# A diffusion layer on one core: the turn from the mixer into the FFN, token tile by token tile

## The chip, the core and the metric

One Trainium2 chip, one of its cores. The core has TensorE (PE, the matrix engine, with its weight loads shown as PEld), VectorE (DVE), ScalarE (ACT), GpSimd (POOL) and SyncE (SP, which here issues the large loads). The engines run their own instruction streams in order and meet through semaphores. The metric is the device time of one launch in microseconds. A run's time is a little longer than the span from its first to its last profiled instruction.

## What is computed

One layer of a diffusion backbone over 256 latent tokens and 256 context tokens of width 2048. The part that this case is about begins at the output projection:

```
x = x + g1 * rms_norm(mix @ w_out, mix_norm_post)
hf = rms_norm(x, ffn_norm_pre) * (1 + sc2) + sh2
x = x + g2 * rms_norm((silu(hf @ w_gate) * (hf @ w_up)) @ w_down, ffn_norm_post)
```

`mix` is what the mixer (gated DeltaNet heads and a conformer branch) leaves, and `g1`, `sc2`, `sh2`, `g2` are columns of a modulation computed from the conditioning vector. `w_out` is 2048 by 2048, `w_gate` and `w_up` are 2048 by 5632, `w_down` is 5632 by 2048. All data are float32.

## The kernel before

**Products in three parts.** Every large product is made of float32r matmuls. Each operand is split into a rounded part (`_hi`) and the remainder (`_lo`), and a product is hi by hi, hi by lo and lo by hi: `product()` (L1774 to L1779) issues three matmuls of 128x512. ScalarE makes the rounded part by a copy (L924), VectorE the remainder by a subtraction (L1325, L1358).

**Weights in units.** Weights come in units of 128 partitions by 1024 columns (512 KB, two k tiles by 512 output columns) through four slots of `raw`, `w_hi` and `w_lo` (`RING = 4`). SP loads a unit as soon as the unit four before it has been split into both parts. A unit can be split into `w_hi` when TensorE has finished the unit four before it. One unit is 12 matmuls on TensorE for the two token tiles (t = 0 and 1, 128 tokens each) and two k tiles.

**The order.** For the mixer and the turn into the FFN there is one list of steps, `PLAN`, built by `make_plan()`. Each engine walks through the whole list and issues the steps that are its own, so the list sets the order on every engine at once. A step waits for others by `need(engine, kind, key)`, a semaphore wait on the count of that kind. Behind the list, each engine runs the FFN loop `gate_up(c, ...)` over 11 chunks of 512 columns, eight units of `w_gate` and eight of `w_up` each, and then the units of `w_down`.

**The turn into the FFN.** Output projection units are named `("wo", c, kg)`: column group c (0 to 3) of 512 columns, kg one of 8 pairs of k tiles. The last column group, c = 3, ends with kg = 0, 1, 2, 3. Token tile t of column group c is accumulated in the PSUM bank 2c + t. Behind it stand these steps:

- `ysq` (ACT, L1205) squares and sums a bank, `ysm` (DVE, L1682) adds the four sums, `yrt` (ACT, L1209) takes the root, `yrc` (DVE, L1686) the reciprocal. `yg` (DVE, L1678) multiplies a bank by the gate and norm weights. `ysq` and `yg` of c = 0 to 2 are done beside the projection.
- `pn` (DVE, L1696) adds the normed bank to the residual `x1`, 8 pieces of 128x512 (t, c).
- `psq` (ACT, L1227), `psm` (DVE, L1682), `xrt` (ACT, L980), `xrc` (DVE, L1363) do the same for the second norm. `xdg` (DVE, L1367) puts the reciprocals on the diagonals `dg`, the matmul `xT` with kp = 8 (PE, L1888) spreads them over the partitions, and `xTc` (ACT, L924) copies them into `rsb`.
- `xT` with kp = 0 to 7 (PE, L1784) transposes `x1`: four 128x128 transposes for each pair kp of k tiles, both token tiles.
- Then for each kp: `fx` (DVE, L1375) multiplies the transposed bank by `rsb` into `hf2`; `fm` (ACT, L1236, two instructions) applies scale and shift in place; `fhi` (ACT, L924) rounds into `h_hi`; `flo` (DVE, L1380) writes the remainder `h_lo`. `hf2` has two buffers, so `fx` of kp waits for `flo` of kp - 2.
- `fh` and `fl` are the two splits of FFN weight unit i (ACT L924, DVE L1325). 0 to 6 stand in the list, the rest in `gate_up`. Unit i = kp of the FFN on TensorE needs `flo` of kp and both splits.

In this version each of these steps serves both token tiles, and the norm of token tile 0 waits for the end of the whole projection: `need(act, "mm", ("wo", c, 3), QS - 1)`. GpSimd does nothing behind its last mixer step but one load of `x1`.

## Time and profile before

| | us |
|---|---|
| median of 3 runs | 1640.35 |
| lowest and highest | 1638.05, 1641.5 |
| the profiled execution | 1639.05 |
| its span | 1637.3 |
| granted TensorE clock, mean over the span | 0.986 |

In the profile an engine's busy time is the union of its instructions. Durations of matmuls are modelled at their ends, so the pace of a stream of matmuls is read from start to start. A row of the timeline gives start, length, engine, line, operation and tiles, the number of instructions merged into it, and in brackets how long the engine had been idle before and what ended that. Tile names in the profile leave out numbers: `x` is `x1`, `hf` is `hf2`, `junk` is `junk2`, `sc` is `sc2`.

### The profile page before, as it was taken

The page shows a single profiled execution, that of the slowest core. Times are in us where ns is not written, and L with a number is a line of the kernel's source. Part 1 is how long each engine was busy: PE and PEld are TensorE (multiplying, and loading weights), DVE is VectorE, ACT ScalarE, POOL GpSimd, SP SyncE. Part 2 cuts the span into 40 slices and gives each one's busy share as a digit, 9 for nine tenths or more (in the row PEclk, how much of TensorE's full clock was granted, in tenths as well). Part 3 has the DMA queues.
Part 4 walks back from the last instruction along what each step waited for, and adds up shares of the span by engine and source line. Part 5 has one row for each costly group of instructions (what it writes and reads, how often), then busy time and mean ns, then how long its engine had stood idle before and what let it go on. Part 6 is the DMA issues. An engine that isn't in the chain of part 4 may idle for free.

```text
span 1637.3 us, 25093 instructions
## 1 busy us (share of the span) xinstructions
PE 1545.0 (94%) x9295; PEld 1298.1 (79%) x9295; DVE 1046.0 (64%) x1446; ACT 768.8 (47%) x1044; POOL 227.5 (14%) x236
## 2 busy tenths in 40 slices
PE   4887999998989999999998999999999999999998
PEld 0557888887878898898876888888888888888886
DVE  1436798999996857675565645544544455777554
ACT  5526633443345645457355644444344444443342
POOL 2000232333332333244200000000000000000000
PEclk9998999999999999999999999999999999999999
DMA  9993555655554555564464666666666665999654
GB/s 355 395 382 97 172 182 184 197 177 196 168 177 158 168 187 196 170 208 130 142 220 127 184 190 192 187 186 190 192 192 186 188 190 176 336 324 322 229 183 139
DMA packets 190977, 334.58 MB, mean 204 GB/s; under 512 B 14706, under 2 KB 80354, under 8 KB 189985
## 3 DMA queue, kind: packets, MB, share of 16 engines
q1 hardware_dynamic: 190194, 330.89, 62.8%
q0 software_dynamic: 688, 2.39, 0.5%
q8 instruction: 63, 1.03, 0.3%
q14 instruction: 32, 0.26, 0.0%
HBM read 331.15 MB, written 2.10 MB: 204 GB/s over the span
## 4 chain that ended last, share of the span: by engine, by line
PE 78%; DVE 11%; DMA 4%; ACT 3%; issue 2%; SPq 2%; DVEq 0%; ACTq 0%
PE PS L1778 64%; DMA first<-in_w_mod_dram 3%; DVE cacc L1639 3%; DVE w_lo L1358 3%; PE PS L1784 2%; PE PS L2086 2%; PE PS L2040 2%; PE PS L1992 2%; SPq L711 2%; DVE sil L1467 1%; PE PS L1938 1%; DVE gh L1525 1%; PE PS L1982 1%; PE PS L1873 1%; DVE xyi L1530 1%
## 5 line engine op out<-in xcount | busy, mean ns | idle before, releaser
L924 ACT ACTIVATE w_hi<-raw 128x1024 fp32r<-128x1024 f32 (+1 forms) x426 | 448.1, 1056 | 513.4 <-PE PS L1778 430.4
L1325 DVE TENSOR_TENSOR w_lo<-raw,w_hi 128x1024 fp32r<-128x1024 f32 x264 | 322.9, 1225 | 316.6 <-ACT w_hi L924 316.5
L1778 PE MATMUL PS<-w_hi,h_hi 128*128 128x512 f32 x704 | 275.0, 391 | 1.9 <-DVE h_lo L1380 1.2
L1778 PE MATMUL PS<-w_hi,h_lo 128*128 128x512 f32 x704 | 274.0, 389 | 0.0
L1778 PE MATMUL PS<-w_lo,h_hi 128*128 128x512 f32 x704 | 273.9, 389 | 0.0
L1358 DVE TENSOR_TENSOR w_lo<-raw,w_hi 128x1024 fp32r<-128x1024 f32 (+1 forms) x162 | 201.4, 1252 | 70.5 <-ACT w_hi L924 70.5
L1778 PE MATMUL PS<-h_hi,w_hi 128*128 128x256 f32 (+1 forms) x784 | 237.6, 303 | 0.0
L1778 PE MATMUL PS<-h_hi,w_lo 128*128 128x256 f32 (+1 forms) x784 | 222.0, 283 | 0.0
L1778 PE MATMUL PS<-h_lo,w_hi 128*128 128x256 f32 (+1 forms) x784 | 221.9, 283 | 0.0
L1778 PEld LDWEIGHTS PS<-h_hi,w_hi 128*128 128x128 f32 (+1 forms) x784 | 148.9, 190 | 36.0 <-issue 27.6
L1778 PEld LDWEIGHTS PS<-w_hi,h_hi 128*128 128x128 f32 x704 | 132.1, 188 | 29.5 <-DVE h_lo L1380 1.4
L1778 PEld LDWEIGHTS PS<-w_hi,h_lo 128*128 128x128 f32 x704 | 132.1, 188 | 27.6
L1778 PEld LDWEIGHTS PS<-w_lo,h_hi 128*128 128x128 f32 x704 | 132.2, 188 | 27.1
L1778 PEld LDWEIGHTS PS<-h_lo,w_hi 128*128 128x128 f32 (+1 forms) x784 | 149.1, 190 | 0.8
L1778 PEld LDWEIGHTS PS<-h_hi,w_lo 128*128 128x128 f32 (+1 forms) x784 | 148.5, 189 | 0.1
L1778 PE MATMUL PS<-w_hi,act_hi 128*128 128x512 f32 x352 | 137.9, 392 | 0.0
L1778 PE MATMUL PS<-w_hi,act_lo 128*128 128x512 f32 x352 | 137.0, 389 | 0.0
L1778 PE MATMUL PS<-w_lo,act_hi 128*128 128x512 f32 x352 | 136.9, 389 | 0.0
L1639 DVE SCALAR_TENSOR_TENSOR cacc<-ub,vcol,cacc 128x196 f32<-128x196 f32 (+14 forms) x240 | 126.2, 585 | 0.2
L873 POOL TENSOR_TENSOR mkl<-kc,lvl 128x512 fp32r<-128x512 f32 x56 | 83.4, 1489 | 155.4 <-PE PS L1982 118.9
L1778 PE MATMUL PS<-hc_hi,w_hi 128*128 128x256 f32 (+1 forms) x272 | 83.8, 308 | 11.5 <-ACT w_hi L924 4.2
L1467 DVE SCALAR_TENSOR_TENSOR sil<-PS,vcol,sil 128x254 f32<-128x254 f32 (+1 forms) x160 | 76.6, 480 | 16.0 <-ACT sil L1044 11.7
(322 smaller groups left out, 2353.7 us busy)
## 6 DMA issues: line engine op xcount, KB each, us to landing
raw<-in_w_in_dram SPq DMA_DIRECT2D x128, 512.0 KB, 3.9
raw<-in_w_mod_dram SPq DMA_DIRECT2D x96, 512.0 KB, 5.0
raw<-in_w_gate_dram SPq DMA_DIRECT2D x88, 512.0 KB, 3.7
raw<-in_w_up_dram SPq DMA_DIRECT2D x88, 512.0 KB, 3.7
raw<-in_w_down_dram SPq DMA_DIRECT2D x88, 512.0 KB, 4.5
first<-in_w_mod_dram SPq DMA_DIRECT2D x64, 512.0 KB, 9.6
raw<-in_w_out_dram SPq DMA_DIRECT2D x32, 512.0 KB, 4.3
gin<-in_w_mod_dram SPq DMA_DIRECT2D x32, 512.0 KB, 6.0
```

What stands on the lines that cost most here:

```text
L711: sp.dma_start(first[:, slot, :].rearrange("p (a b) -> p a b", a=2), w_mod_v[:, 2 * j:2 * j + 2, part * D + q * 512:part * D + (q + 1) * 5 ...
L873: pool.tensor_tensor(mkl[:, :, :, :].rearrange("p t h c -> p (t h) c"), kc[:, :, :, :].bitcast(F32).rearrange("p t h c -> p (t h) c"), bc( ...
L924: act.activation(out_ap, in_ap, ACT.Copy).then_inc(S[kind], 1)
L1325: dve.tensor_tensor(w_lo[:, slot, :], raw[:, (R0 + n) % RING, :], w_hi[:, slot, :].bitcast(F32), ALU.subtract).then_inc(S["lo"], 1)
L1358: dve.tensor_tensor(lo, raw[:, at_ring[u] % RING, 0:sz], hi.bitcast(F32), ALU.subtract).then_inc(done, 1)
L1467: ins = dve.scalar_tensor_tensor(out=o, in0=pr[:, T * h + a + off:T * h + b + off], scalar=vcol[:, col:col + 1], in1=o, op0=ALU.mult, op1= ...
L1639: ins = dve.scalar_tensor_tensor(out=dst, in0=src, scalar=vcol[:, col:col + 1], in1=dst, op0=ALU.mult, op1=ALU.add)
L1778: ins = pe.matmul(out_ap, a[i], b[j], start=start and n == 0, stop=stop and n == 2, skip_group_check=grouped)
L1784: ins = pe.transpose(PS[:, bank_, P * n:P * (n + 1)], src, ident[:, :])
L1992: ins = pe.matmul(PS[:, b, P * n:P * (n + 1)], a, m, start=False, stop=True, skip_group_check=True)
L2040: ins = pe.matmul(PS[:, b, P * n:P * (n + 1)], a, m, start=True, stop=True)
L2086: ins = pe.matmul(PS[32 * tile:32 * tile + 1, 3, :], csil[:, LAT, j:j + 1], raw[:, n % RING, 512 * h:512 * (h + 1)], start=j == 0, stop=j ...
```

## The change

The first norm, the second norm, the transposes and the modulation are made for token tile 0 and token tile 1 apart. The last four projection units (c = 3, kg = 0 to 3) first run their token tile 0 halves (parts 0 and 2 of each), all four, and then, in the new list, their token tile 1 halves (parts 1 and 3); `ysq 0 3` waits for the token tile 0 halves alone. The steps of the turn are no longer built by loops but read from a written list `INTO_FFN`, 148 steps, in which the third token of an `xT`, `fx`, `fm`, `fhi`, `flo` is the token tile. `fx`, `fhi` and `flo` become twice as many instructions of 128x(2x128), `fm` twice as many of 128x128. FFN units 0 to 3 are computed by a new step `ft` on TensorE, one for each unit and token tile (6 matmuls). The remainders of FFN weight units 1 to 3 are made by GpSimd in a new step `gl`; each waits for the rounding of its own unit and for the remainder before it, and VectorE's remainder of unit 4 waits for the last of them.

Transposed pairs now use half a bank for each pair: kp 0 and 1 of tile t in bank 6 + t, kp 2 and 3 in 2 + t, 4 and 5 in 4 + t, 6 and 7 in 6 + t again. `xT` of kp 6 and 7 waits for both `fx 0` and `fx 1` of its tile.

```diff
-TURNED = (6, 7, 2, 3, 4, 5, 6, 7, 1)
+TURNED = (6, 6, 2, 2, 4, 4, 6, 6, 0)
+BY_TILE = 4
...
-        unit(("wo", c, kg), QS)
+        u = ("wo", c, kg)
+        if c == 3 and kg < BY_TILE:
+            plan.extend([("hi", (u,)), ("lo", (u,))] + [("mm", (u, half * NT)) for half in range(2)])
+            continue
+        unit(u, QS)
...
-    plan.extend([(k, (i,)) for i in range(3) for k in ("fh", "fl")])
-    plan.extend([("ysq", (t, 3)) for t in range(NT)] + [("ysm", ()), ("yrt", ()), ("fh", (3,))])
-    plan.extend([("yg", (t, 3)) for t in range(NT)] + [("yrc", ())])
-    plan.extend([(k, (t, c)) for c in (3, 0, 1, 2) for t in range(NT) for k in ("pn", "psq")])
-    plan.extend([("xT", (FFN, kp)) for kp in range(6)])
-    plan.extend([("psm", ()), ("xrt", (FFN,)), ("xrc", (FFN,)), ("xdg", ())])
-    plan.extend([("xT", (FFN, 8)), ("xTc", (FFN, 8)), ("fx", (FFN, 0)), ("fm", (FFN, 0)), ("fhi", (FFN, 0)), ("fx", (FFN, 1)),
-                 ("xT", (FFN, 6)), ("xT", (FFN, 7))])
-    for kp in range(8):
-        plan.append(("flo", (FFN, kp)))
-        plan.extend([("fm", (FFN, kp + 1)), ("fhi", (FFN, kp + 1))] if kp < 7 else [])
-        plan.extend([("fx", (FFN, kp + 2))] if kp < 6 else [])
-        if kp == 1:
-            plan.append(("fl", (3,)))
-        elif kp in SPLIT_AT:
-            plan.extend([("fh", (SPLIT_AT.index(kp) + 4,)), ("fl", (SPLIT_AT.index(kp) + 4,))])
+    plan.extend(into_ffn())
...
+INTO_FFN = """
+    ysq 0 3, ysm 0, yrt 0, yg 0 3, yrc 0, mm 0 1, mm 0 3, mm 1 1, xT 0 0, mm 1 3, mm 2 1, mm 2 3, mm 3 1, mm 3 3,
+    xT 8 0, xT 1 0, fh 0, pn 0 3, psq 0 3, pn 0 0, psq 0 0, fh 1, pn 0 1, psq 0 1, pn 0 2, psq 0 2, ysq 1 3, psm 0,
...
+                elif kind == "gl":
+                    i, = key
+                    pool.wait_ge(S["hi"], B0 + i + 1)
+                    pool.wait_ge(S["lo"], B0 + i)
+                    slot = (B0 + i) % RING
+                    pool.tensor_tensor(w_lo[:, slot, :], raw[:, (R0 + i) % RING, :], w_hi[:, slot, :].bitcast(F32),
+                                       ALU.subtract).then_inc(S["lo"], 1)
...
-                    need(act, "mm", ("wo", c, 3), QS - 1)
-                    n = COUNT[kind, key] - 1
+                    need(act, "mm", ("wo", c, 3), NT + t)
+                    n = SQUARED.index((kind, key))
                     if n >= 4:
-                        act.wait_ge(S[kind], n - 3)
+                        need(act, SQUARED[n - 4][0], *SQUARED[n - 4][1])
...
+                    _, kp, t = key
+                    need(act, "fx", FFN, kp, t)
                     need(act, "s2")
                     for k in range(2):
                         kt = 2 * kp + k
-                        ins = act.activation(hf2[:, kp % 2, k, :], hf2[:, kp % 2, k, :], ACT.Identity, scale=sc2[:, kt:kt + 1],
+                        part = hf2[:, kp % 2, k, P * t:P * (t + 1)]
+                        ins = act.activation(part, part, ACT.Identity, scale=sc2[:, kt:kt + 1],
                                              bias=modc[:, KT + kt:KT + kt + 1])
                     ins.then_inc(S[kind], 1)
                 elif kind == "fhi":
-                    _, kp = key
-                    need(act, "fm", FFN, kp)
-                    copy(h_hi[:, 2 * kp:2 * kp + 2, :], hf2[:, kp % 2, :, :], kind)
+                    _, kp, t = key
+                    need(act, "fm", FFN, kp, t)
+                    tok = slice(P * t, P * (t + 1))
+                    copy(h_hi[:, 2 * kp:2 * kp + 2, tok], hf2[:, kp % 2, :, tok], kind)
...
+                if n == BY_TILE:
+                    dve.wait_ge(S["lo"], B0 + n)
...
-                    need(dve, "xrc", FFN)
-                    for t in range(NT):
-                        ins = dve.tensor_scalar(dg[:, t, :], ident[:, :], rstd[:, 4 + t:5 + t], None, ALU.mult)
-                    ins.then_inc(done, 1)
+                    t, = key
+                    need(dve, "xrc", FFN, t)
+                    dve.tensor_scalar(dg[:, t, :], ident[:, :], rstd[:, 4 + t:5 + t], None, ALU.mult).then_inc(done, 1)
                 elif kind == "fx":
-                    _, kp = key
-                    need(dve, "xT", FFN, kp)
-                    need(dve, "xTc", FFN, 8)
+                    _, kp, t = key
+                    need(dve, "xT", FFN, kp, t)
+                    need(dve, "xT", FFN, kp ^ 1, t)
+                    need(dve, "xTc", FFN, 8, t)
                     if kp >= 2:
-                        need(dve, "flo", FFN, kp - 2)
-                    dve.tensor_tensor(hf2[:, kp % 2, :, :], PS[:, TURNED[kp], :].rearrange("p (k t) -> p k t", k=2),
-                                      bc(rsb[:, :], 1, 2), ALU.mult).then_inc(done, 1)
+                        need(dve, "flo", FFN, kp - 2, t)
+                    tok = slice(P * t, P * (t + 1))
+                    src = PS[:, TURNED[kp] + t, T * (kp % 2):T * (kp % 2 + 1)].rearrange("p (k t) -> p k t", k=2)
+                    dve.tensor_tensor(hf2[:, kp % 2, :, tok], src, bc(rsb[:, tok], 1, 2), ALU.mult).then_inc(done, 1)
                 elif kind == "flo":
-                    _, kp = key
-                    need(dve, "fhi", FFN, kp)
-                    dve.tensor_tensor(h_lo[:, 2 * kp:2 * kp + 2, :], hf2[:, kp % 2, :, :],
-                                      h_hi[:, 2 * kp:2 * kp + 2, :].bitcast(F32), ALU.subtract).then_inc(done, 1)
+                    _, kp, t = key
+                    need(dve, "fhi", *key)
+                    tok = slice(P * t, P * (t + 1))
+                    dve.tensor_tensor(h_lo[:, 2 * kp:2 * kp + 2, tok], hf2[:, kp % 2, :, tok],
+                                      h_hi[:, 2 * kp:2 * kp + 2, tok].bitcast(F32), ALU.subtract).then_inc(done, 1)
...
-                    need(dve, *(("ysq", 1, 3) if kind == "ysm" else ("psq", 1, 2)))
-                    a, o = (8, 6) if kind == "ysm" else (16, 4)
-                    dve.tensor_reduce(sums[:, o:o + 2], sums[:, a:a + 8].rearrange("p (t c) -> p t c", t=NT), AX_X,
-                                      ALU.add).then_inc(done, 1)
+                    t, = key
+                    need(dve, *(("ysq", t, 3) if kind == "ysm" else ("psq", t, 2)))
+                    a, o = (8 + 4 * t, 6 + t) if kind == "ysm" else (16 + 4 * t, 4 + t)
+                    dve.tensor_reduce(sums[:, o:o + 1], sums[:, a:a + 4], AX_X, ALU.add).then_inc(done, 1)
...
+                    if key[0] == FFN:
+                        _, kp, t = key
+                        b = TURNED[kp] + t
+                        if kp == 8:
+                            need(pe, "xdg", t)
+                            need(pe, "pn", t, 0)
+                            pe.matmul(PS[:, b, 0:P], ones[:, :], dg[:, t, :], start=True, stop=True).then_inc(done, 1)
+                            continue
+                        need(pe, "pn", t, kp // 2)
+                        if kp < 2:
+                            need(pe, "pn", t, 3)
+                        if kp >= 6:
+                            need(pe, "fx", FFN, 0, t)
+                            need(pe, "fx", FFN, 1, t)
+                        for k in range(2):
+                            ins = pe.transpose(PS[:, b, T * (kp % 2) + P * k:T * (kp % 2) + P * (k + 1)],
+                                               x1[:, t, P * (2 * kp + k):P * (2 * kp + k + 1)], ident[:, :])
+                        ins.then_inc(done, 1)
+                        continue
...
+                elif kind == "ft":
+
+                    i, t = key
+                    slot, tok = (B0 + i) % RING, slice(P * t, P * (t + 1))
+                    pe.wait_ge(S["hi"], B0 + i + 1)
+                    pe.wait_ge(S["lo"], B0 + i + 1)
+                    need(pe, "flo", FFN, i, t)
+                    need(pe, "xTc", FFN, 8, t)
+                    for k in range(2):
+                        col, kt = slice(512 * k, 512 * (k + 1)), 2 * i + k
+                        ins = product(PS[:, t, :], (h_hi[:, kt, tok], h_lo[:, kt, tok]), (w_hi[:, slot, col], w_lo[:, slot, col]),
+                                      512, kt == 0, False)
+                    if t == NT - 1:
+                        ins.then_inc(f_mm, 1)
...
+                        if i < BY_TILE:
+                            continue
                         if i < 8:
-                            need(pe, "flo", FFN, i)
-                            need(pe, "xTc", FFN, 8)
+                            for t in range(NT):
+                                need(pe, "flo", FFN, i, t)
```

ScalarE, from the squares of the last projection bank on. Before (`w_hi<-raw` are weight splits, `junk2,sums` are `ysq` on a bank and `psq` on `x1`, the `rtmp` rows `yrt` and `xrt`):

```order
L1205 ACTIVATE junk2,sums<-PS 128x512 x2
L1209 ACTIVATE rtmp<-sums,cst 128x2
L924 ACTIVATE w_hi<-raw 128x1024
L1227 ACTIVATE junk2,sums<-x1 128x512 x8
L980 ACTIVATE rtmp<-sums,cst 128x2
L924 ACTIVATE rsb<-PS 128x256
L1236 ACTIVATE hf2<-hf2,modc,sc2 128x256 x2
L924 ACTIVATE h_hi<-hf2 128x512
```

and now:

```order
L1236 ACTIVATE junk2,sums<-PS 128x512
L1241 ACTIVATE rtmp<-sums,cst 128x1
L950 ACTIVATE w_hi<-raw 128x1024
L1256 ACTIVATE junk2,sums<-x1 128x512 x2
L950 ACTIVATE w_hi<-raw 128x1024
L1256 ACTIVATE junk2,sums<-x1 128x512 x2
L1236 ACTIVATE junk2,sums<-PS 128x512
L1011 ACTIVATE rtmp<-sums,cst 128x1
L1241 ACTIVATE rtmp<-sums,cst 128x1
L950 ACTIVATE rsb<-PS 128x128
L950 ACTIVATE w_hi<-raw 128x1024
L1266 ACTIVATE hf2<-hf2,modc,sc2 128x128 x2
```

Three weight splits (units 0, 1 and 2) that stood ahead of the first row before now stand behind it, between the steps of the two norms, and the root of token tile 0's second norm stands behind the square of token tile 1's last projection bank.

VectorE, from the sum of `ysq` to the first `h_lo`. Before:

```order
L1682 TENSOR_REDUCE sums<-sums 128x2
L1678 TENSOR_TENSOR PS<-PS,gw_all 128x512 x2
L1686 RECIPROCAL rstd<-rtmp 128x2
L1696 SCALAR_TENSOR_TENSOR x1<-PS,rstd,x1 128x512 x8
L1682 TENSOR_REDUCE sums<-sums 128x2
L1363 RECIPROCAL rstd<-rtmp 128x2
L1367 TENSOR_SCALAR dg<-ident,rstd 128x128 x2
L1375 TENSOR_TENSOR hf2<-PS,rsb 128x512 x2
L1380 TENSOR_TENSOR h_lo<-hf2,h_hi 128x512
```

and now, from the second sum of token tile 0 on:

```order
L1719 TENSOR_REDUCE sums<-sums 128x1
L1358 TENSOR_TENSOR w_lo<-raw,w_hi 128x1024
L1719 TENSOR_REDUCE sums<-sums 128x1
L1714 TENSOR_TENSOR PS<-PS,gw_all 128x512
L1397 RECIPROCAL rstd<-rtmp 128x1
L1723 RECIPROCAL rstd<-rtmp 128x1
L1401 TENSOR_SCALAR dg<-ident,rstd 128x128
L1733 SCALAR_TENSOR_TENSOR x1<-PS,rstd,x1 128x512
L1411 TENSOR_TENSOR hf2<-PS,rsb 128x2x128 x2
L1733 SCALAR_TENSOR_TENSOR x1<-PS,rstd,x1 128x512 x2
L1416 TENSOR_TENSOR h_lo<-hf2,h_hi 128x2x128
```

The remainder of weight unit 0 and token tile 1's first norm now stand between the second sum of token tile 0 and its diagonal.

TensorE, at the end of the projection (`hc_` operands) and the start of the FFN (`h_` operands). Before:

```order
L1778 MATMUL PS<-w_hi,hc_lo 128x512
L1784 MATMUL PS<-ident,x1 128x128 x24
L1888 MATMUL PS<-dg,ones 128x256
L1784 MATMUL PS<-ident,x1 128x128 x8
L1778 MATMUL PS<-w_hi,h_hi 128x512
```

and now, where the last projection matmul is followed by:

```order
L1815 MATMUL PS<-w_hi,hc_lo 128x512
L1926 MATMUL PS<-dg,ones 128x128
L1935 MATMUL PS<-ident,x1 128x128 x14
L1815 MATMUL PS<-w_hi,h_hi 128x512
```

Two transposes of token tile 0 (`xT 0 0`) are moved up into the projection, 15 matmuls (two and a half units' token tile 1 halves) ahead of its end, and the other 14 of that tile stand behind the matmul that needs the diagonal; the 16 of token tile 1 are spread among the `ft` steps.

## Rows read from the trace of the kernel before

**Rows 1.** The page: busy time by engine; a weight load with its time to landing.

```profile
PE 1545.0 (94%) x9295; PEld 1298.1 (79%) x9295; DVE 1046.0 (64%) x1446; ACT 768.8 (47%) x1044; POOL 227.5 (14%) x236
...
raw<-in_w_gate_dram SPq DMA_DIRECT2D x88, 512.0 KB, 3.7
```

**Rows 2.** The chain of waits behind the turn: start, length, engine and line.

```profile
912.00 46.50 PE PS L1778 x204
```

**Rows 3.** Timeline of TensorE through the turn.

```profile
882.35 0.39 PE L1778 MATMUL PS<-w_hi,hc_lo 128*128 128x512 f32 x1
...
888.33 4.76 PE L1784 MATMUL PS<-ident,x 128*128 128x128 f32 x24 [5.59 <-DVE x L1696]
...
895.02 1.23 PE L1784 MATMUL PS<-ident,x 128*128 128x128 f32 x8 [1.36 <-DVE hf L1375]
897.44 0.50 PE L1778 MATMUL PS<-w_hi,h_hi 128*128 128x512 f32 x1 [1.20 <-DVE h_lo L1380]
...
912.00 0.47 PE L1778 MATMUL PS<-w_hi,h_hi 128*128 128x512 f32 x1 [0.66 <-DVE w_lo L1325]
```

**Rows 4.** Stretches: length, busy time (instructions) by engine, granted clock, DMA.

```profile
882.80:912.00 29.20, 20.46 (x95) 16.87 (x95) 20.57 (x34) 23.46 (x50) 0.00 (x0) 0.88 0.20 57
...
885.40:888.30 2.90, 0.00 (x0) 0.00 (x0) 2.87 (x7) 2.08 (x7) 0.00 (x0) 0.51 0.08 30
888.30:892.20 3.90, 3.87 (x18) 3.87 (x19) 2.77 (x5) 3.66 (x12) 0.00 (x0) 0.50 0.00 0
892.20:893.70 1.50, 1.46 (x10) 0.94 (x8) 0.65 (x3) 0.00 (x1) 0.00 (x0) 0.97 0.00 0
```

**Rows 5.** Groups of instructions from 882 to 914 us, ScalarE: busy, mean ns.

```profile
L1236 ACT ACTIVATE hf<-hf,modc,sc 128x256 f32<-128x256 f32 x16 | 8.7, 591 | 2.7 <-DVE hf L1375 2.7
...
L924 ACT ACTIVATE w_hi<-raw 128x1024 fp32r<-128x1024 f32 x5 | 5.1, 1043 | 0.0
L924 ACT ACTIVATE h_hi<-hf 128x512 fp32r<-128x512 f32 x8 | 5.1, 632 | 0.3
L1227 ACT ACTIVATE junk<-x 128x512 f32<-128x512 f32 x8 | 5.0, 631 | 0.8 <-DVE x L1696 0.8
```

**Rows 6.** The same groups, VectorE.

```profile
L1375 DVE TENSOR_TENSOR hf<-PS,rsb 128x512 f32<-128x512 f32 x8 | 5.4, 690 | 2.1 <-ACT rsb L924 1.3
L1380 DVE TENSOR_TENSOR h_lo<-hf,h_hi 128x512 fp32r<-128x512 f32 x8 | 5.4, 685 | 1.4 <-ACT h_hi L924 1.2
L1696 DVE SCALAR_TENSOR_TENSOR x<-PS,rstd,x 128x512 f32<-128x512 f32 x8 | 5.4, 741 | 0.0
```

**Rows 7.** Timeline of ScalarE and VectorE through the turn.

```profile
882.78 0.60 ACT L1205 ACTIVATE junk<-PS 128x512 f32<-128x512 f32 x1 [1.60 <-PE PS L1778]
...
885.55 5.36 DVE L1696 SCALAR_TENSOR_TENSOR x<-PS,rstd,x 128x512 f32<-128x512 f32 x8
...
894.91 1.09 ACT L1236 ACTIVATE hf<-hf,modc,sc 128x256 f32<-128x256 f32 x2 [0.83 <-DVE hf L1375]
...
896.03 0.63 ACT L924 ACTIVATE h_hi<-hf 128x512 fp32r<-128x512 f32 x1
...
896.57 1.08 ACT L1236 ACTIVATE hf<-hf,modc,sc 128x256 f32<-128x256 f32 x2
...
911.60 0.63 ACT L924 ACTIVATE h_hi<-hf 128x512 fp32r<-128x512 f32 x1
```

**Rows 8.** Groups of ScalarE over the span, small pieces: busy, mean ns.

```profile
L1131 ACT ACTIVATE gmv<-kn 128x128 f32<-128x128 f32 x32 | 9.5, 297 | 0.2
```

**Rows 9.** One line each: durations min/median/max in ns, first and last start.

```profile
L880 POOL TENSOR_TENSOR mlo<-mn,mhi x16: 1288/1402/1737, 230.7 to 784.1; 128x512 fp32r<-128x512 f32 x16
...
L1637 DVE TENSOR_SCALAR cacc<-ub,vcol x8: 338/348/1385, 158.2 to 422.2; 128x256 f32<-128x256 f32 x8
```

**Rows 10.** Timeline of GpSimd and VectorE at 561 us.

```profile
560.91 1.28 POOL L873 TENSOR_TENSOR mkl<-kc,lvl 128x512 fp32r<-128x512 f32 x1 [6.55 <-DVE pi L1512]
561.04 2.24 DVE L1358 TENSOR_TENSOR w_lo<-raw,w_hi 128x1024 fp32r<-128x1024 f32 x1 [0.20 <-ACT w_hi L924]
```

88 lines of the change are left out of this document (50 added, 38 removed).

## Prediction

> **What bounds the kernel now.** I read the page first, then the chain of waits, then the turn into the FFN engine by engine. TensorE is busy for 94% of the span [rows 1], and from 912.00 us on the chain is TensorE alone, 204 matmuls in 46.50 us [rows 2], 0.227 us from start to start, 2.72 us for a unit of 12. So before and behind the turn the kernel is bound by TensorE, and the change can move the end only by moving the moment from which TensorE streams without a gap. I take the start of FFN unit 8 as the mark, the first that needs weights alone. Five units (0 to 4) are computed before 912.00, so it now starts at 912.00 + 3 x 2.72 = 920.16.
>
> The last projection matmul ends at 882.35 + 0.39 = 882.74 [rows 3]. In the 37.4 us from there to the mark TensorE must do 8 units, 21.8 us, and 32 transposes; 8 of them at full clock took 1.23, so all take at most 4.9. The rest, 10.7 us, is all that a perfect turn could give back (0.65%). The timeline names 8.8 of it: 5.59 waiting for the residual, 1.36 for `fx`, 1.20 for the first remainder, 0.66 for the remainder of weight unit 5 [rows 3]. The clock has most of the rest: from 885.4, 2.7 us behind the last matmul, to 892.2 the granted clock is 0.5, its 1.2 GHz level, and 24 transposes take 4.76 [rows 3, 4].
>
> The engine next to the limit is ScalarE. In the 29.2 us of the turn it is busy for 23.46, VectorE for 20.57 [rows 4]. That is what I look at in the change.
>
> **Part by part: token tile 0 starts early.** The times below come from a walk through the new order by hand: each step starts when the one ahead of it on its engine is through and what it waits for has ended, at the durations of the rows. Eight half-unit parts of 0.68 us stay behind the squares of tile 0's last bank. Its `ysq` starts at 882.78 - 8 x 0.68 + 0.16 (the last matmul's tail) = 877.50 instead of 882.78 [rows 7]. Sum, root and scaling take 1.6, so `pn 0 3` is at 879.1 and `pn 0 0` ends 1.4 later at 880.5 (0.74 long, 0.66 apart [rows 6, 7]). TensorE has meanwhile reached `xT 0 0`, after three parts, at 879.5, and waits 1.0 there; the transposes add 0.2. The projection therefore ends at 884.3 instead of 882.74.
>
> **The second norm of tile 0 is held three times.** ScalarE runs in order. `psq 0 1` stands behind weight split 1, which needs projection unit 1's last matmul (881.6) and takes 0.95 (1.04 long, 0.09 overlapped [rows 5]); the fourth `psq` ends at 884.0. The root stands behind `ysq 1 3`, which waits for the end of the projection: 885.2. On VectorE the reciprocal stands behind weight remainder 0 and tile 1's `yg`: 885.9. The diagonal could start at 886.1.
>
> **GpSimd's remainders.** The trace has no 128x1024 on GpSimd. The nearest row is the same subtraction at 128x512, 1.29 at least and 1.40 in the median [rows 9], so I take twice that, 2.6 (bounds 2.4 and 3.5). Nothing in the old turn shows how it gets on with VectorE, but the mixer does. A GpSimd operation from 560.91 to 562.19 overlaps a VectorE remainder that starts at 561.04 and takes 2.24 instead of 1.22 [rows 10]: it lost the rest of the other's run. A `tensor_scalar` that takes 0.34 takes up to 1.39 [rows 9]. The first `gl` starts at 885.4, when weight remainder 0 is ready, and ends at 888.0: the diagonal, a `tensor_scalar`, waits 1.9. The second (from 890.0) holds tile 0's first `flo` 1.4, the third (from 894.7) holds `flo 2 0` 1.4. What is saved, 3 x 1.14 on VectorE, is saved on an engine that was idle for 8.6 of the 29.2. The price of GpSimd alone is 2.0 us at the mark in my walk, bounds 0 and 3.9.
>
> The Trainium skill, SBUF — State Buffer, Who interferes with whom, says that a VectorE instruction with two SBUF inputs, or in a two-port mode, and a GpSimd instruction that reads SBUF exclude each other for the whole instruction. By it the walk stands at +3.6 us; without it, at +1.5. The trace agrees: 2.24 against 1.22.
>
> **Tile 0 goes on.** Diagonal 888.3, spread 888.7, copy 889.0, `fx 0 0` 889.1. ScalarE has weight split 2 ahead, so `fm` runs from 889.9, `fhi` ends at 891.2, `flo` (held) at 893.06. `ft 0 0` starts at 893.1, where unit 0 now starts at 897.44 [rows 3]: 4.3 ahead. The idle time before it is 4.0 + 0.2 + 2.5.
>
> **Half pieces do not cost half.** This decides. One kp now occupies ScalarE from 894.91 to 896.57, 1.66 us: `fm` pair, `fhi` at 896.03 [rows 7]. From 512 to 1024 columns a copy grows by 0.41 (632 to 1043 ns [rows 5]), 0.8 ns a column. Half the width thus takes only 0.10 off each `fm` (0.59 to 0.49, 0.39 to the next) and 0.2 off `fhi` (0.33 to the next); a half piece costs 0.39 + 0.49 + 0.03 + 0.33 = 1.23 with rounding. A 128x128 instruction at 0.297 [rows 8] shows the same: it is mostly not columns. Sixteen of them take 19.7 where eight took 13.3: 6.4 us more on ScalarE. Besides, seven weight splits now stand ahead of the last `fhi` behind that first `ysq`, where three did: 3.8 more. VectorE's `fx` and `flo` grow alike, 0.35 against 0.61 to the next, but VectorE has room.
>
> **The sum.** ScalarE starts at 877.50 with 23.5 + 6.4 + 3.8 = 33.7 of work, and about 0.5 for doubled roots and copies. Never idle, it would end at 911.7. But it waits 7.1: 1.2 in the first norms, 3.0 for the spread diagonal of tile 0, 0.2 + 1.1 + 0.6 for tile 1's root, diagonal and first `fx`, 0.75 for `fx 6 0`, 0.2 in pieces. The last `fhi` ends at 919.0 (now 911.60 + 0.63 = 912.2 [rows 7]). Weight split 7 ends at 920.0, its remainder at 921.2, unit 7 starts at 921.3, unit 8 at 924.0. The same walk over the old order, by the same durations, gives 920.45 where the trace has 920.16, so I count 3.6 of the difference. Behind the mark nothing is taken back, since TensorE stays without a gap. Loads are covered: unit 7's is issued when the third `gl` ends at 897.4 and needs 3.7 [rows 1], and ScalarE asks at 918.9.
>
> **The clock.** TensorE idles 4.0 us from 884.3 on, longer than the 2.7 after which the clock fell before [rows 4]. I expect it to fall again. Half speed up to 896 costs 0.2, since waits cover it, up to 898 1.0, up to 903 3.4. I add 0.6. The sum is +4.2 us on the profiled execution, 1639.05 + 4.2 = 1643.3; the median stands 1.3 above that execution, which gives 1644.5.
>
> **Rivals.**
> - *The clock stays low* until past 903 us, because TensorE then works in pieces of 1 to 3 us with gaps of 1 to 2.5. For it: it took 3.9 us of dense work to return before. Against: at half speed the gaps close. +6 to +8.5, 1648.
> - *GpSimd is not in the way*, its remainders fall beside PSUM reads of VectorE or run faster. `ft 0 0` at 889.8, mark at 922.0, +1.5: 1641.9. Rows 10 speak against it.
> - *Faster: ScalarE keeps up.* If a half piece costs half (0.83 us, the point from which TensorE is last again), TensorE streams from `ft 0 0`: 893.1 + 21.8 + 16 transposes at 0.15 = 917.3, 2.9 before today's mark, and 6.2 before it if GpSimd does not hold either. 1634 to 1637.5. For it: the early start is real. Against it: the 0.8 ns a column. The Trainium skill, ScalarE: Activation LUTs, What ACT_TABLE_LOAD costs, gives an ACTIVATE 186 ns plus 0.833 a column plus 93 for each pointer operand, by which `fm` at 128 columns takes 0.48. The trace's 0.59 at 256 agrees.
> - *The walk is off by the waits it cannot see*, with order and mechanism right, and half of ScalarE's 7.1 us of waiting goes: 0 to +2.5, 1641.5.
>
> **How the numbers follow.** A measurement of this kernel tells 0.2% (3.3 us, from 1637.1 to 1643.6) from no change. Forecast 0.48, of which 0.40 lies above 1643.6; low clock 0.15; no exclusion 0.17; fewer waits 0.10; faster 0.10. Slower is 0.40 + 0.15 = 0.55, same 0.08 + 0.17 + 0.10 = 0.35, faster 0.10. The range takes in all but the faster case and the end of the low clock: 1639.5 to 1649.5.
>
> **What would show it.** In the new profile: GpSimd's three subtractions of about 2.6 us, and beside each a VectorE instruction on `dg` or `h_lo` stretched by 1 to 2 us; the first `h_` matmul near 893; ScalarE's `hf` instructions at 0.49 us, nearly without idle time from 901 to 919; unit 5 to 7 matmuls waiting for remainders that wait for ScalarE; a half clock behind 887. The forecast is wrong if `hf` pieces take under 0.4 us, if no VectorE instruction is stretched, or if TensorE streams without a gap before 912.

## The result, and the profile after

Median 1643.37 us (1639.10 to 1646.94, 19 runs) against 1639.62 (1634.94 to 1642.19, 19 runs) for the kernel before on the same chip; the ratio is 1.0025 with a 95% interval of 1.0016 to 1.0034. The change makes the kernel slower by about 4 us. The profiled execution has a span of 1642.0 us where the old one had 1637.3. The page of the changed kernel, which answers to [rows 1]:

```profile
PE 1546.7 (94%) x9297; PEld 1297.4 (79%) x9297; DVE 1048.1 (64%) x1463; ACT 774.6 (47%) x1071; POOL 235.1 (14%) x239
```

TensorE's work is unchanged, ScalarE has 5.8 us more, GpSimd three instructions more. The end of the turn, in the chain of waits (start, length, what), which answers to [rows 2]:

```profile
919.64 1.05 ACT w_hi L950
920.69 0.02 issue
920.71 1.24 DVE w_lo L1358
921.95 0.14 issue
922.09 41.07 PE PS L1815 x180
```

TensorE streams only from 922.09, from unit 7 on, so unit 8 starts at 922.09 + 2.72 = 924.81 instead of 920.16: 4.65 later, and the span is 4.7 longer. Everything happens ahead of that mark. TensorE in the turn (first bracket: idle time before it and what ended it), which answers to [rows 3]:

```profile
880.32 0.44 PE L1935 MATMUL PS<-ident,x 128*128 128x128 f32 x2 [1.06 <-DVE x L1733]
...
883.82 0.39 PE L1815 MATMUL PS<-w_hi,hc_lo 128*128 128x512 f32 x1
887.78 0.80 PE L1926 MATMUL PS<-dg,ones 128*128 128x128 f32 x2 [3.58 <-DVE dg L1401]
888.37 3.19 PE L1935 MATMUL PS<-ident,x 128*128 128x128 f32 x14
892.83 0.77 PE L1815 MATMUL PS<-w_hi,h_hi 128*128 128x512 f32 x1 [1.26 <-DVE h_lo L1416]
...
903.61 0.47 PE L1815 MATMUL PS<-w_hi,h_hi 128*128 128x512 f32 x1 [1.33 <-DVE h_lo L1416]
...
909.82 0.47 PE L1815 MATMUL PS<-w_hi,h_hi 128*128 128x512 f32 x1 [1.40 <-DVE h_lo L1416]
...
918.70 0.47 PE L1815 MATMUL PS<-w_hi,h_hi 128*128 128x512 f32 x1 [1.52 <-DVE w_lo L1358]
...
922.09 0.47 PE L1815 MATMUL PS<-w_hi,h_hi 128*128 128x512 f32 x1 [0.41 <-DVE w_lo L1358]
```

The first FFN product comes 4.6 us earlier than before (892.83 against 897.44), and the lead is lost in four later waits (1.33, 1.40, 1.52 and 0.41, 4.66 together), to the half clock and to tile 1's transposes, which now stand among the products. Two stretches (length, busy time and instructions of PE, PEld, DVE, ACT, POOL, then granted clock), which answer to [rows 4]:

```profile
882.50:912.00 29.50, 21.94 (x94) 17.48 (x93) 19.01 (x38) 22.70 (x58) 7.08 (x3) 0.83 0.31 89
887.80:897.40 9.60, 8.34 (x29) 7.09 (x30) 7.29 (x11) 8.65 (x22) 4.75 (x2) 0.50 0.44 128
```

The granted clock is at half for nearly 10 us, where it was for 6.8. GpSimd's subtractions and the VectorE instructions beside them:

```profile
885.31 2.33 POOL L844 TENSOR_TENSOR w_lo<-raw,w_hi 128x1024 fp32r<-128x1024 f32 x1 [56.88 <-DVE w_lo L1358]
...
885.93 1.80 DVE L1401 TENSOR_SCALAR dg<-ident,rstd 128x128 f32<-128x128 f32 x1
...
889.92 2.37 POOL L844 TENSOR_TENSOR w_lo<-raw,w_hi 128x1024 fp32r<-128x1024 f32 x1 [2.27 <-ACT w_hi L950]
...
891.09 1.48 DVE L1416 TENSOR_TENSOR h_lo<-hf,h_hi 128x256 fp32r<-128x256 f32 x1
...
894.52 2.38 POOL L844 TENSOR_TENSOR w_lo<-raw,w_hi 128x1024 fp32r<-128x1024 f32 x1 [2.23 <-ACT w_hi L950]
...
895.69 1.48 DVE L1416 TENSOR_TENSOR h_lo<-hf,h_hi 128x256 fp32r<-128x256 f32 x1 [1.24 <-ACT h_hi L950]
```

The diagonal takes 1.80 and ends 0.09 after GpSimd's first subtraction (885.31 + 2.33 = 887.64). The two `h_lo` end 0.27 to 0.28 after the second and third. ScalarE late in the turn, which answers to [rows 7], one half piece of it and the last copy:

```profile
909.57 0.87 ACT L1266 ACTIVATE hf<-hf,modc,sc 128x128 f32<-128x128 f32 x2
910.47 0.42 ACT L950 ACTIVATE h_hi<-hf 128x256 fp32r<-128x256 f32 x1
910.79 1.05 ACT L950 ACTIVATE w_hi<-raw 128x1024 fp32r<-128x1024 f32 x1
...
919.32 0.42 ACT L950 ACTIVATE h_hi<-hf 128x256 fp32r<-128x256 f32 x1
```

A half piece occupies ScalarE from 909.57 to 910.79, 1.22 us, where a whole one took 1.66. The last copy starts at 919.32 and ends at 919.74. Its groups from 877 to 922 us (busy, mean ns, then idle time before them), which answer to [rows 5]:

```profile
L1266 ACT ACTIVATE hf<-hf,modc,sc 128x128 f32<-128x128 f32 x32 | 13.9, 480 | 1.3 <-DVE hf L1411 1.3
...
L950 ACT ACTIVATE h_hi<-hf 128x256 fp32r<-128x256 f32 x16 | 6.6, 416 | 0.4
```

### The profile page after: what moved, and what is told of

The parts are those of the page before. It is cut to its first block, busy times and chain, and to the rows that moved or that the text cites. A ratio compares the mean times of both kernels' runs of the same rounds, so it can differ in the third digit from the quotient of the medians.

```text
span 1642.0 us, 25203 instructions
## 1 busy us (share of the span) xinstructions
PE 1546.7 (94%) x9297; PEld 1297.4 (79%) x9297; DVE 1048.1 (64%) x1463; ACT 774.6 (47%) x1071; POOL 235.1 (14%) x239
## 4 chain that ended last, share of the span: by engine, by line
PE 78%; DVE 12%; ACT 3%; issue 3%; DMA 2%; SPq 2%; DVEq 0%; ACTq 0%
PE PS L1815 64%; DVE cacc L1675 3%; DVE w_lo L1391 3%; DMA first<-in_w_mod_dram 2%; PE PS L1821 2%; PE PS L2129 2%; PE PS L2083 2%; PE PS L2035 2%; DVE sil L1503 1%; SPq L730 1%; PE PS L1981 1%; PE PS L1910 1%; DVE gh L1561 1%; PE PS L2025 1%; ACT w_hi L950 1%
## 5 line engine op out<-in xcount | busy, mean ns | idle before, releaser
L1358 DVE TENSOR_TENSOR w_lo<-raw,w_hi 128x1024 fp32r<-128x1024 f32 x261 | 319.3, 1225 | 309.8 <-ACT w_hi L950 309.7
```

What stands on the lines that cost most here:

```text
L1358: dve.tensor_tensor(w_lo[:, slot, :], raw[:, (R0 + n) % RING, :], w_hi[:, slot, :].bitcast(F32), ALU.subtract).then_inc(S["lo"], 1)
```

## The experiments

**How they are read.** The spans of profiled executions also differ by up to 7 us ahead of the turn, where all kernels have the same code: tile 0's square of the third chunk (`ysq 0 2`) starts at 856.91 in one and at 864.11 in another. So I give the start of unit 8 as if that square had started at 861.96, as in the changed kernel. Behind unit 8 nothing differs: span less unit 8 is 717.1 to 717.2 in both kernels of this study, and where TensorE no longer waits before unit 8 I take it as span less 717.2. The fourth column is the walk of the prediction, written as a program with measured durations (GpSimd 2.36 us) and without clock losses; the program itself is not shown here. "Filler" is matmuls that nobody reads, "whole" is pieces 4 to 7 of the modulation made for both tiles at once.

| kernel | span | unit 8, aligned | walk | ratio of times to before |
|---|---|---|---|---|
| before | 1637.3 | 920.1 | 920.5 | |
| changed | 1642.0 | 924.8 | 923.6 | 1.0025 (1.0016 to 1.0034) |
| changed, remainders on VectorE | 1638.4 | 922.0 | 922.0 | 1.0005 (0.9993 to 1.0017) |
| before, remainders on GpSimd | 1636.0 | 919.3 | 919.6 | 1.0002 (0.9989 to 1.0015) |
| changed, filler | 1640.6 | 923.6 | 923.6 | 1.0015 (1.0005 to 1.0025) |
| changed, pieces 4 to 7 whole | 1639.5 | 922.7 | 922.8 | 1.0018 (1.0008 to 1.0027) |
| reordered, half pieces | 1632.4 | 916.4 | 915.2 | 0.9976 (0.9961 to 0.9991) |
| reordered, pieces 4 to 7 whole | 1630.2 | 913.5 | 913.6 | 0.9950 (0.9935 to 0.9965) |
| the same, filler | 1625.6 | 913.5 | 913.6 | 0.9941 (0.9920 to 0.9962) |
| three steps moved | 1637.6 | 922.1 | 919.7 | 1.0015 (1.0001 to 1.0028) |
| whole, VectorE, own order | 1633.4 | 914.1 | 913.7 | 0.9969 (0.9957 to 0.9981) |
| reordered halves, filler | 1632.3 | 915.2 | 915.2 | 0.9962 (0.9949 to 0.9974) |
| reordered whole, on VectorE | 1635.9 | 916.7 | 916.0 | 0.9981 (0.9970 to 0.9992) |
| three moved, filler | 1637.4 | 919.8 | 919.7 | 0.9993 (0.9980 to 1.0007) |

Each mark comes from one profiled execution, so it holds the clock's behaviour of that execution. The timings bear the marks out as a whole: in all thirteen rows below the first, the distance of the mark from 920.1, as a share of the time, lies in the interval of the ratio. They don't resolve single steps of 1 to 2 us: 1.0015 and 1.0018 (filler, and pieces 4 to 7 whole, in the changed kernel) and 1.0015 (three moves) overlap with 1.0025, and what is said below of such steps rests on the profiles. The two kernels with the smallest ratios have 5 and 4 runs, the other experiments 9 or 10.

**GpSimd's part, undone and alone.** The first puts the three subtractions back on VectorE in the changed kernel, the second puts them on GpSimd in the kernel before. In the first, VectorE's remainder of unit 4 no longer waits for GpSimd's last, and its line is left out below.

```diff
-                elif kind == "gl":
...
-                    pool.tensor_tensor(w_lo[:, slot, :], raw[:, (R0 + i) % RING, :], w_hi[:, slot, :].bitcast(F32),
-                                       ALU.subtract).then_inc(S["lo"], 1)
...
-                elif kind == "fl":
+                elif kind in ("fl", "gl"):
```

> The changed kernel with the weight remainders of FFN units 1 to 3 subtracted on VectorE again, at the same places of the order; nothing is left out. Theory (GpSimd's three subtractions keep VectorE's SBUF operations out): the diagonal takes 0.28 us instead of 1.80, the two h_lo steps 0.42 instead of 1.48 each, the first FFN product of tile 0 starts near 890 instead of 892.83, and the start of FFN unit 8 moves 1.5 to 2 us earlier (walk: 1.5), span near 1640.4. Rival (the stretched operations end beside other waits, so their cost does not reach the end): unit 8 within 0.4 us of 924.8, since VectorE now carries three subtractions of about 1.2 us itself. Second rival: those subtractions cost VectorE more than the exclusion did, and unit 8 is up to 2 us later.

```diff
-    plan.extend([(k, (i,)) for i in range(3) for k in ("fh", "fl")])
+    plan.extend([(k, (i,)) for i in range(3) for k in ("fh", "gl" if i else "fl")])
...
-            plan.append(("fl", (3,)))
+            plan.append(("gl", (3,)))
```

> The kernel before with one part of the change alone: the remainders of FFN units 1 to 3 on GpSimd, the turn in its old order; nothing is left out. Theory: the operations of VectorE that run beside them read PSUM, so few are stretched; VectorE is rid of about 3.6 us, but ScalarE's chain sets the end, and unit 8 starts 0 to 0.7 us earlier than in the kernel before (920.16). Rival (GpSimd's part is what makes the changed kernel slower, through the exclusion): unit 8 is 1.5 us or more later than 920.16.

With the remainders on VectorE, VectorE's diagonal and `h_lo`, and TensorE's first FFN product:

```profile
885.12 0.29 DVE L1392 TENSOR_SCALAR dg<-ident,rstd 128x128 f32<-128x128 f32 x1
...
888.46 0.42 DVE L1407 TENSOR_TENSOR h_lo<-hf,h_hi 128x256 fp32r<-128x256 f32 x1
...
889.14 0.77 PE L1806 MATMUL PS<-w_hi,h_hi 128*128 128x512 f32 x1 [0.75 <-DVE h_lo L1407]
```

The stretching is gone and unit 8 comes 2.8 us earlier, more than the 1.5 to 2 I gave. The walk explains 1.6. The other 1.2 is as much as the clock costs the changed kernel (next run); here it was at half too, from about 887 to 893, but the mark stands where the walk puts it without a loss. That the 1.2 is the clock's is worked out in this way and not shown by a run of its own. In the kernel before, the same three subtractions do no harm, 0.8 earlier and not later (I gave 0 to 0.7). GpSimd's third there, and VectorE's instructions beside it:

```profile
885.01 5.36 DVE L1705 SCALAR_TENSOR_TENSOR x<-PS,rstd,x 128x512 f32<-128x512 f32 x8
...
885.05 2.36 POOL L825 TENSOR_TENSOR w_lo<-raw,w_hi 128x1024 fp32r<-128x1024 f32 x1 [1.96 <-ACT w_hi L931]
```

Eight `pn` in 5.36 us, exactly as in [rows 7]: they read PSUM and one SBUF operand, and GpSimd does not hold them. The same three subtractions on GpSimd cost 2.8 us in one order and gain 0.8 in the other. The gain of 0.8 is seen in the profile only; the timing (1.0002) doesn't resolve it.

**The clock.** Matmuls that nobody reads keep TensorE at work.

```diff
- mm 3 3, xT 8 0,
+ mm 3 3, fill 0, xT 8 0,
...
- xT 7 0, ft 0 0,
+ xT 7 0, fill 1, ft 0 0,
...
+                    for _ in range((13, 7)[n]):
+                        pe.matmul(PS[:, (2, 0)[n], :], hc_hi[:, 0, 0:P],
+                                  hc_hi[:, 2:4, :].rearrange("p k t -> p (k t)"), start=True, stop=True)
```

> The changed kernel with 13 more matmuls of 128x512 after the last projection product, and 7 more after the transposes of tile 0, into PSUM banks that are free there and that nobody reads; they only keep TensorE at work where it waited. Nothing is left out. Theory (the half clock between 887 and 897 costs the start of FFN unit 8 about 1.0 us): the granted clock stays at 1.00 through that stretch, the transposes take about 1.6 us instead of 3.19, and unit 8 starts about 1.0 us earlier, near 923.8. Rival (the half clock only stretches work that waits anyway): unit 8 within 0.3 us of 924.8.

The stretch of the half clock, with filler (here PE alone, then granted clock):

```profile
887.50:892.00 4.50, 3.83 (x23) 1.00 0.53 165
892.00:898.00 6.00, 4.67 (x23) 1.00 0.39 98
```

The clock stayed at 1.00 and unit 8 came 1.2 us earlier. So the half clock cost 1.2 us of the end. The chain of waits shows where the loss passes. In the changed kernel it runs through tile 0's products on TensorE, then through the matmul that spreads tile 1's diagonal and its copy `rsb` on ScalarE:

```profile
892.83 2.90 PE PS L1815 x6
...
900.45 0.24 PE PS L1926 x2
900.71 0.29 ACT rsb L950
```

Six products take 2.90 us there at the half clock. With filler the copy stands earlier:

```profile
899.31 0.29 ACT rsb L950
```

That is 899.52 aligned, 1.19 earlier, so the whole difference at the mark is there already. With the remainders on VectorE the same copy is at 897.11, aligned 897.91, 2.8 earlier. From this copy to unit 8 it takes 24.1 us in all three.

**Half pieces.** Pieces 4 to 7 of `fm`, `fhi` and `flo` are made for both tiles at once again.

```diff
- fx 4 0, flo 2 1, ft 2 1, fm 3 1, fh 4, fm 4 0, fhi 3 1, ft 3 1, fx 4 1, fl 4, fhi 4 0, flo 4 0,
+ flo 2 1, ft 2 1, fm 3 1, fh 4, fhi 3 1, ft 3 1, fx 4 2, fl 4, flo 3 1, fm 4 2, fhi 4 2, flo 4 2,
...
-                        part = hf2[:, kp % 2, k, P * t:P * (t + 1)]
+                        part = hf2[:, kp % 2, k, span(t)]
```

> The changed kernel with the pieces 4 to 7 of the modulated activations made for both token tiles at once again (VectorE's multiply still as two instructions, since the two tiles lie in two banks; ScalarE's two scales and copy, and VectorE's subtraction, whole). Nothing is left out. Theory (half pieces cost ScalarE 1.22 us each against 1.66 for a whole, and ScalarE sets the end): ScalarE is rid of 4 x 0.8 = 3.2 us, and unit 8 starts 2 to 3 us earlier, 922 to 923. Rival (PE or VectorE sets the end after 912, not ScalarE): unit 8 within 0.5 us of 924.8.

Unit 8 is 2.1 us earlier, as expected, but not all of it is the pieces. Up to tile 1's copy `rsb` this kernel has the steps of the changed one, and the copy already stands at 899.41, aligned 899.86, 0.85 earlier: in this execution the clock was at half only from about 892.3 to 895.7. From there to the mark it takes 22.8 instead of 24.1, so the pieces are worth 1.3 here (the walk has 0.8). The same steps thus met the half clock for about 10 us in one execution and for 3.4 in another. With the clock kept at 1.00 and each in its own good order (below), whole pieces are worth 915.2 - 913.5 = 1.7 us.

**The order.** Walk and trace are within 0.3 us of each other in these four runs, and 1.2 apart in the changed kernel, as much as the filler gave back there. So I let the program look for a better order of the same steps. The sum of the second norm then has to wait for whichever of its four squares is last.

```diff
- mm 1 1, xT 0 0, mm 1 3, mm 2 1, mm 2 3, mm 3 1, mm 3 3, xT 8 0, xT 1 0, fh 0, pn 0 3, psq 0 3, pn 0 0, psq 0 0, fh 1,
+ mm 1 1, mm 1 3, mm 2 1, mm 2 3, mm 3 1, mm 3 3, xT 3 0, xT 2 0, xT 8 0, fh 0, pn 0 0, psq 0 0, pn 0 1, psq 0 1, psq 0 2,
...
-                    need(dve, *(("ysq", t, 3) if kind == "ysm" else ("psq", t, 2)))
+                    need(dve, *(("ysq", t, 3) if kind == "ysm" else LAST_PSQ[t]))
```

> The changed kernel with the same steps written in another order (the list of the turn alone is rewritten, and the sum of the second norm waits for the last of its four squares); half pieces and GpSimd's three remainders stay as they are. Nothing is left out. The order comes from a walk by hand-measured durations, made by program: a step starts when its engine is free and its inputs are there, and GpSimd's subtraction keeps VectorE's operations on two SBUF operands waiting. That walk gives 923.6 for the changed kernel without its clock loss (the filler run measured 923.4), 922.0 for the remainders on VectorE (measured 921.2, or 922.0 when both start their turn at the same time) and 922.8 for the whole pieces (measured 922.2, or 922.7). Theory (the changed kernel is late by the order of its steps, not by half pieces and GpSimd in themselves): FFN unit 8 starts at 915.2 with the clock high, up to 2 us later with it at half after the waits of 2.5 and 1.4 us that remain; so 915 to 917.5, 7 to 9.5 us earlier than 924.8 and 3 to 5 us earlier than in the kernel before, span 1632 to 1635. Rival (the half pieces and GpSimd set the end whatever the order): unit 8 no earlier than 922.

Unit 8 came at 916.4, 8.5 us earlier than in the changed kernel and 3.7 earlier than in the one before, with all half pieces and all of GpSimd's work. The rival falls. Then the same with pieces 4 to 7 whole; this is its list:

```
ysq 0 3, ysm 0, yrt 0, yg 0 3, yrc 0, mm 0 1, mm 0 3, mm 1 1, mm 1 3, mm 2 1, mm 2 3, mm 3 1, mm 3 3, xT 8 0,
xT 0 0, xT 1 0, fh 0, pn 0 2, psq 0 2, pn 0 0, fh 1, psq 0 0, pn 0 3, psq 0 3, pn 0 1, psq 0 1, ysq 1 3, fl 0,
xrt 0, psm 0, yg 1 3, xrc 0, fh 2, xT 3 0, xT 3 1, xT 5 0, xT 2 0, ysm 1, xdg 0, yrc 1, yrt 1, fh 3, pn 1 0,
pn 1 1, pn 1 2, pn 1 3, fx 0 0, psm 1, gl 1, xTc 8 0, psq 1 0, psq 1 1, psq 1 2, psq 1 3, fm 0 0, xrt 1,
xT 1 1, xT 5 1, xT 2 1, xT 7 0, xT 6 0, xT 0 1, fx 1 0, xrc 1, xdg 1, flo 0 0, gl 2, fx 2 0, gl 3, fx 0 1,
fhi 0 0, fm 1 0, xTc 8 1, fhi 1 0, fm 2 0, fm 0 1, xT 4 0, xT 8 1, flo 1 0, fhi 0 1, fx 3 0, fx 1 1, ft 0 0,
ft 1 0, xT 6 1, xT 4 1, xT 7 1, fhi 2 0, flo 0 1, flo 2 0, fm 1 1, fm 3 0, fx 2 1, ft 0 1, flo 1 1, fhi 1 1,
fm 2 1, fx 3 1, ft 2 0, ft 1 1, ft 3 0, flo 3 0, fhi 3 0, fhi 2 1, flo 2 1, ft 2 1, fm 3 1, fhi 3 1, fh 4,
ft 3 1, fx 4 2, flo 3 1, fx 5 2, fm 4 2, fhi 4 2, fl 4, flo 4 2, fl 5, fh 5, fm 5 2, fhi 5 2, fx 6 2, flo 5 2,
fh 6, fm 6 2, fx 7 2, fl 6, fhi 6 2, flo 6 2, fm 7 2, fhi 7 2, flo 7 2
```

> As the reordered kernel, with pieces 4 to 7 made whole for both tiles (as in the run of whole pieces) and an order of its own from the same walk. Nothing is left out. Theory (whole pieces are worth about as much in a good order as in the old one, where they gave 2.2 us): unit 8 at 913.6 by the walk with the clock high; TensorE waits 2.8 us in one piece before the diagonal and then has dense work from 891, so the half clock costs the end 1 to 2.5 us here: 914.6 to 916. Rival (ScalarE is no longer what sets the end, and whole pieces give nothing): unit 8 at or later than in the reordered kernel.

TensorE's one long wait, GpSimd's three subtractions and the diagonal beside them, the end of the chain, and a stretch with its clock:

```profile
884.88 0.78 PE L1940 MATMUL PS<-dg,ones 128*128 128x128 f32 x2 [2.69 <-DVE dg L1405]
```

```profile
882.39 7.37 POOL L848 TENSOR_TENSOR w_lo<-raw,w_hi 128x1024 fp32r<-128x1024 f32 x3 [54.43 <-DVE w_lo L1362]
```

```profile
884.09 0.74 DVE L1405 TENSOR_SCALAR dg<-ident,rstd 128x128 f32<-128x128 f32 x1
```

```profile
890.48 3.05 PE PS L1829 x12
893.53 0.66 PE PS L1949 x6
894.19 57.17 PE PS L1829 x252
```

```profile
886.00:890.00 4.00, 3.86 (x25) 3.65 (x24) 3.08 (x9) 4.00 (x14) 3.62 (x2) 0.71 0.76 226
```

From 890.48 on TensorE never waits. Its list has all four splits `fh 0` to `fh 3` on ScalarE ahead of tile 1's `psq`, where ScalarE would wait for them. GpSimd runs its three in one piece while VectorE is in `pn`, which it does not hold; only the diagonal loses, 0.74 instead of 0.28. I expected 914.6 to 916 because of the clock; it was 913.5, the walk's value without any loss. The next run says the same of the clock.

```diff
- mm 3 3, xT 8 0,
+ mm 3 3, fill 0, xT 8 0,
...
+FILL = ((12, 4, ('pn', 0, 2)), (2, 4, ('pn', 0, 2)), (2, 0, ('xTc', 2, 8, 0)), (2, 0, ('xTc', 2, 8, 0)))
```

> The kernel of the run before with 18 more matmuls of 128x512 that nobody reads, in PSUM banks that are free: 12 before the diagonal of tile 0, and three times 2 in the short waits behind it. Nothing is left out. Theory (the half clock costs this order 1 to 2.5 us, since its products are dense from 891 on): the granted clock stays at 1.00 and unit 8 starts at 913.6 to 914.2, span 1630.5 to 1632. Rival (the clock costs nothing that was not waited for anyway): within 0.3 us of the run before.

Its rival holds: unit 8 moved by less than 0.1, and the 1 to 2.5 us that I gave the clock were not there. The shorter span (1625.6) lies ahead of the turn, which began 4.6 us earlier in that execution, and the intervals of the two ratios overlap. In this order the clock was at half only while transposes ran ahead of what they waited for. Both kernels beat the one before by 0.5 to 0.6%.

**Three steps of the order.** From the changed kernel, the program's single moves with the largest gain.

```diff
- mm 1 1, xT 0 0, mm 1 3, mm 2 1, mm 2 3, mm 3 1, mm 3 3, xT 8 0,
+ mm 1 1, mm 1 3, mm 2 1, mm 2 3, mm 3 1, mm 3 3, xT 0 0, xT 8 0,
...
- psq 0 0, fh 1, pn 0 1, psq 0 1, pn 0 2, psq 0 2, ysq 1 3, psm 0, xrt 0, fl 0, ysm 1, yg 1 3, yrt 1, xT 3 0,
+ psq 0 0, pn 0 1, psq 0 1, pn 0 2, psq 0 2, ysq 1 3, psm 0, xrt 0, fl 0, ysm 1, yg 1 3, yrt 1, fh 1, xT 3 0,
...
- fm 5 1, fhi 5 1,
+ fm 5 1, fh 6, fhi 5 1,
...
- fx 7 1, fh 6, fl 6,
+ fx 7 1, fl 6,
```

> The changed kernel with three of its steps at other places and nothing else: the split fh 1 on ScalarE after the root yrt 1 (behind tile 0's squares and tile 1's), the transposes xT 0 0 on TensorE behind the last projection product, and the split fh 6 five steps of ScalarE earlier. Nothing is left out. All times are counted as if the third square of tile 0 started at 861.96, as in the changed kernel. Theory (the order of single steps is what made the changed kernel later than the one before): the walk gives unit 8 at 919.7 where it gives 923.6 for the changed kernel, 1.8 of it for fh 1, 1.25 for xT 0 0, 0.9 for fh 6; with the clock loss of 0 to 1.2, 919.7 to 921. Rival (the reordered kernels gained by many small moves, or by something the walk does not hold, and these three give less than 1.5 us together): 923.3 or later.

> The kernel with three moved steps, with 21 matmuls of 128x512 that nobody reads, in free PSUM banks: 8 before the diagonal of tile 0 and 13 before the first FFN product. Nothing is left out. With the three moves alone unit 8 stood at 922.1 by the alignment, 2.7 us earlier than in the changed kernel but 2.4 later than the walk's 919.7, and the granted clock was at half from about 884 to 894. Theory (the missing 2.2 us is the clock, so the three moves are worth 3.9 us against the changed kernel with its clock kept up, 923.6): 919.7 to 920.2 with the clock at 1.00. Rival (the walk lacks a wait in this order, and the clock's loss lay beside other waits): 921.5 to 922.2 with the clock at 1.00.

The three moves alone gave 922.1: 2.7 us, which neither the theory's 919.7 to 921 nor the rival's 923.3 took in. With filler (8 matmuls before `xT 8 0`, 13 before `ft 0 0`) it was 919.8, as the walk has it. A stretch with three moves alone, and the same with filler (PE, then clock):

```profile
886.00:890.00 4.00, 1.21 (x4) 0.50 0.59 150
```

```profile
886.00:890.00 4.00, 3.74 (x23) 1.00 0.49 140
```

So the moves are worth 923.6 - 919.8 = 3.8 us, and 2.3 of that was hidden by the clock. What each of the three is worth (1.8, 1.25 and 0.9) is the walk's division; no run has one of them alone.

**What the parts are worth in a good order.**

```diff
+FILL = ((3, 4, ('pn', 0, 2)), (10, 4, ('pn', 0, 2)), (6, 0, ('xTc', 2, 8, 0)))
```

> The reordered kernel with half pieces, with 19 matmuls of 128x512 that nobody reads in its three waits (3, 10 and 6, in free PSUM banks). Nothing is left out. In that kernel unit 8 stood at 916.35 by the alignment (915.23 as read), where the walk gave 915.2 plus 0.2, the walk's usual distance, and the granted clock was 0.50 from 886 to 890 and 0.79 to 894. Theory (the missing 1.0 to 1.2 us is the clock): the clock stays at 1.00 and unit 8 comes at 915.2 to 915.5. Rival (a wait that the walk lacks): 916.0 to 916.6 with the clock at 1.00.

The clock stayed at 1.00 and unit 8 came at 915.2: the missing 1.1 us of the reordered kernel was the clock. The last two put GpSimd's remainders back on VectorE: once in the order of the reordered whole kernel (the edit of the first experiment), once in an order found for that.

> The reordered kernel with whole pieces 4 to 7, in the same order, with the remainders of units 1 to 3 subtracted on VectorE. Nothing is left out. Theory (GpSimd's part loses through the exclusion only where two-SBUF operations of VectorE fall beside it; in this order one does, by 0.4, so here it saves VectorE's time): unit 8 2.4 us LATER than with GpSimd, 915.5 to 916.5 by the alignment, where the same undoing made the changed kernel 2.8 us earlier. Rival (the exclusion costs more than it saves in every order): unit 8 at 913.4 or earlier.

> Pieces 4 to 7 whole, all weight remainders on VectorE, and an order that the walk found for just this set of steps. Nothing is left out. Theory (with a fitting order GpSimd's three remainders are worth nothing): the walk gives unit 8 at 913.7 against 913.6 with GpSimd; TensorE waits 1.0, 2.5 and 0.85 us on the way, so the half clock may add up to 1.2: 913.6 to 915 by the same alignment. Rival (VectorE's 3.6 us more of work set the end): 916 or later.

In GpSimd's order the undoing costs 3.2 us (916.7 against 913.5, just outside the 915.5 to 916.5 that I gave; the walk has 2.4, and the clock was at half again, from about 888 to 898, which may be the rest). In its own order it costs 0.6 (914.1), of which the walk has 0.1, inside the expected 913.6 to 915. GpSimd's part, then, is worth little where the order is made for its absence.

## Why the prediction was right

The forecast was 1644.5, slower by 4.15; it came out slower by 3.75, inside the range. Of the 1.1 us between 1644.5 and 1643.37, 0.7 is the starting point: the median of three runs of the old kernel, 1640.35, where 19 runs have 1639.62. At the mark the forecast was 3.6 later and 0.6 of clock; measured it is 3.5 with the clock kept up (923.6 against 920.1) and 1.2 of clock. The steps, each against the new trace:

- Tile 0's first square: 877.50 forecast, 877.26. TensorE's wait before `xT 0 0`: 1.0, 1.06. End of the projection: 884.3, 884.2.
- Diagonal held by GpSimd: 1.9 from 886.1, took 1.80 from 885.93 (1.5 of it held). The two `flo`: 1.4 each forecast, 1.06 each. The subtraction takes 2.33 to 2.38, below my 2.6 and just under the lower bound of 2.4. `ft 0 0`: 893.1, 892.83.
- GpSimd's price of 2.0 at the mark: 2.8 by the undoing, 1.6 against the filler run. The walk without it had `ft 0 0` at 889.8 and the mark at 922.0; with the remainders on VectorE they are at 889.9 (889.14 as read) and 922.0.
- Half piece 1.23, measured 1.22; `fm` at 128 columns 0.49, measured 0.48. The Trainium skill, ScalarE: Activation LUTs, What ACT_TABLE_LOAD costs, gives an estimate of 0.48 for it (186 ns, 0.833 a column, 93 for each of two pointer operands), and the trace agrees. The last `fhi` was to end at 919.0 and ends at 919.74, unit 7 at 921.3 starts at 922.09: both 0.7 to 0.8 late, since the forecast added the clock only at the end. Unit 8 at 924.0 plus 0.6 of clock, 924.81.
- ScalarE's work and waiting: 34.2 and 7.1 forecast, from 877.26 to 919.74 it was busy for 33.8 and idle for 8.7. The largest miss is tile 1's root, diagonal and first `fx`, 1.9 forecast and 2.9 measured (0.23 + 2.09 + 0.59), which is where the half clock passes.
- The clock fell again, at 887 and until 897, and I gave it 0.6 where it cost 1.2: the one term of the sum that was off by a factor of two. I had priced half speed up to 896 at 0.2 and up to 898 at 1.0. The order of sizes was right, but "waits cover it" held for less of it than I took.
- Of the rivals, "GpSimd is not in the way" would have needed instructions without stretching; the trace shows three stretched. "The walk is off by the waits it cannot see" wanted half of ScalarE's waiting to go; it waited 8.7 and not 3.5. "The clock stays low" beyond 903 did not happen.

One point misplaced the cause, and the forecast of the time did not depend on it. "Half pieces do not cost half. This decides." The arithmetic under it held to 0.01 us, but half pieces do not decide: with half pieces everywhere the turn can end at 915.2, 4.9 before the old kernel's mark. What the sum contained without naming its worth was the order. The prediction saw that `psq 0 1` stands behind weight split 1 (one of its "held three times") and that TensorE waits at `xT 0 0`, and left both there as part of the walk; these places with `fh 6` carry 3.8 us, more than half pieces (1.3 to 1.7 for four of the eight), exclusion (1.6) or clock (1.2). They overlap, so they don't add up to the 4.65. And the rival "faster" made a cheap half piece its condition. That condition was wrong: in the reordered kernel with half pieces and filler, TensorE waits only 0.29 us ahead of `ft 0 0` and 0.16 behind it. That it is the place of the weight splits, where ScalarE would wait, that allows this is read from the list and the walk; no run moves them alone.

Not tried: the kernel before with a better order of its own steps. The walk finds no order of them that starts unit 8 before 918.8, 1.7 ahead of its 920.5 for the old order; TensorE waits there for the whole norm of both tiles. If that holds, tile by tile is what makes 913.5 possible, but no run shows it. So the runs compare the old kernel in its first order with the new steps in a searched one.

## What to carry to other kernels

The order over several in-order engines can be worth more than all of the edits that came with it: write the walk (durations from one trace, in-order engines, waits), see that it gives the known kernels within some tenths, and only then judge an idea, each time in an order made for it. The walk here has no clock in it and was up to 2.4 us too early where the clock fell; with the clock kept up by filler it was within 0.1 us in all four kernels. Work handed to GpSimd was free here beside VectorE instructions with one operand in PSUM (`pn`), and cost time beside its diagonals and remainders (`dg`, `h_lo`), whose operands all lie in SBUF: place it beside the first kind, or leave it out. Measure the moment that bounds the end, relative to a point just ahead of the edit, since the whole span moved by more for other reasons than by most of these edits.

## What the hardware showed unexpectedly

- Between VectorE and GpSimd the one that comes second waits. In the rows of the turn GpSimd came first: VectorE's small diagonal waited 1.5 us, while GpSimd's single subtractions took 2.33 to 2.41. In the mixer of the old kernel it is the other way round:

```profile
549.71 0.68 DVE L1611 TENSOR_TENSOR hc_lo<-ub,hc_hi 128x512 fp32r<-128x512 f32 x1
549.87 2.81 POOL L861 TENSOR_TENSOR kc<-mn 128x512 fp32r<-128x512 f32 x1 [9.58 <-DVE mn L1501]
550.31 1.22 DVE L1358 TENSOR_TENSOR w_lo<-raw,w_hi 128x1024 fp32r<-128x1024 f32 x1
```

  GpSimd's addition, 1.29 at the least, takes 2.81, and VectorE's two instructions take their usual 0.68 and 1.22. So GpSimd can lose time by the overlap as well, which the turn alone does not show. Eight `pn`, with PSUM and SBUF operands, ran in 5.36 us beside GpSimd, unchanged. By the Trainium skill, SBUF — State Buffer, Who interferes with whom, two SBUF inputs (or a two-port mode) on VectorE are what counts, and these rows agree.
- A half clock has no fixed price. It cost 1.2 us in the changed kernel, 2.3 with three steps moved, 1.1 with half pieces reordered, and less than 0.1 with whole pieces reordered, where transposes fell into it and not FFN products. Each figure is the difference of two single executions, and how long the clock stayed down differed between executions with the same steps. Where a better order lost to it (the three moves), filler matmuls gave the loss back.
- Ahead of the turn, with the same code, the profiled executions differ by 7.2 us (the square at 856.91 and 864.11), more than most effects studied here. I did not look for the cause.
